# Modulation sums of a two-layer decoder trunk: four placed at the norms, a section's products moved into the mixer of layer 0

## The reference, cut to what matters

```python
c_act = jax.nn.silu(c)
for l in range(DEPTH):                       # DEPTH = 2
    mod = (c_act @ ada_w[l] + ada_b[l])[:, None, :]
    sh1, sc1, g1, sh2, sc2, g2 = jnp.split(mod, 6, axis=-1)
    h = rmsnorm(x, norm_mix_w[l]) * (1.0 + sc1) + sh1
    x = x + g1 * hybrid_mixer(h, ...)        # w_in, three branches with sigmoid gates, merged @ w_o
    h = rmsnorm(x, norm_ffn_w[l]) * (1.0 + sc2) + sh2
    ffn = swiglu(h, ...) if l % 2 == 0 else moe_swiglu(h, ...)   # top 2 of 8 experts
    x = x + g2 * ffn
return rmsnorm(x, final_norm_w)
```

## Time and profile before

| | |
|---|---|
| median of 3 runs | 1588.82 us (1588.61 to 1588.83) |
| the profiled execution | 1589.61 us, span 1586.9 us |
| busy: PE, PEld, DVE, ACT, POOL | 96%, 83%, 82%, 60%, 2% of the span |
| mean granted TensorE clock | 0.978 of full speed |
| DMA | 469.00 MB, mean 296 GB/s |
| stages by PE's matmuls | mixer 0 to 308 us, dense FFN to 520, mixer 1 to 789, experts to the end |

### The profile page before, as it was taken

One profiled execution on the slowest core, in us unless ns is written; L12 is line 12 of the kernel. 1 busy time (PEld: TensorE's weight loads), 2 busy tenths in 40 slices (PEclk: granted clock), 3 DMA queues, 4 the chain that ended last, 5 costly groups with the idle time before them and its releaser, 6 DMA issues.

```text
span 1586.9 us, 26455 instructions
## 1 busy us (share of the span) xinstructions
PE 1528.8 (96%) x9638; PEld 1322.0 (83%) x9638; DVE 1294.7 (82%) x1508; ACT 957.9 (60%) x1104; POOL 39.5 (2%) x46
## 2 busy tenths in 40 slices
PE   6899999899999899999889999999999999999997
PEld 5898999899999898999877777777777777777775
DVE  7776878767764878868669989899899998989897
ACT  3434544444433533544368777787878777787784
POOL 0000000000000000000002000000000000000200
PEclk7899999999999999999979999999999999999999
DMA  9943878468976543789549999999999999999993
GB/s 348 295 143 107 264 254 287 152 194 293 305 300 196 167 144 128 259 287 375 194 124 385 395 388 396 383 377 370 382 364 388 372 379 381 363 386 368 392 391 147
DMA packets 260624, 469.00 MB, mean 296 GB/s; under 512 B 15732, under 2 KB 129580, under 8 KB 260548
## 3 DMA queue, kind: packets, MB, share of 16 engines
q1 hardware_dynamic: 257024, 456.75, 81.3%
q0 software_dynamic: 3248, 11.11, 1.9%
q10 hardware_dynamic: 276, 0.09, 0.0%
HBM read 453.90 MB, written 14.00 MB: 295 GB/s over the span
## 4 chain that ended last, share of the span: by engine, by line
PE 75%; DVE 4%; issue 1%; ACT 0%; DVEq 0%
PE psU L621 52%; PE psA L621 22%; PE psA L1033 1%; DVE split L1332 1%; DVE merged L1441 0%; PE psU L971 0%; PE psU L993 0%; DVE rstd L1437 0%; DVE split L1813 0%; DVE adacc L1404 0%; DVE sc L1567 0%; DVE work L1635 0%; DVE work L2017 0%; DVE work L1551 0%; DVE work L1544 0%
## 5 line engine op out<-in xcount | busy, mean ns | idle before, releaser
L1116 ACT ACTIVATE split<-raw 128x1024 fp32r<-128x1024 f32 x754 | 787.5, 1059 | 364.8 <-PE psU L621 180.3
L1813 DVE TENSOR_TENSOR split<-raw,split 128x1024 fp32r<-128x1024 f32 x528 | 615.2, 1219 | 22.7 <-ACT split L1116 20.7
L621 PE MATMUL psU<-hS,split 128*128 128x256 f32 x3936 | 490.2, 287 | 18.1 <-DVE hS L1518 14.7
L621 PEld LDWEIGHTS psU<-hS,split 128*128 128x128 f32 x3936 | 483.5, 195 | 20.9 <-issue 16.8
L621 PE MATMUL psU<-split,xE 128*104 128x512 f32 (+1 forms) x2304 | 498.1, 376 | 2.3 <-DVE xE L1940 2.3
L621 PEld LDWEIGHTS psU<-split,xE 128*104 128x104 f32 x2304 | 366.9, 168 | 120.2 <-issue 2.4
L1332 DVE TENSOR_TENSOR split<-raw,split 128x1024 fp32r<-128x1024 f32 x226 | 268.8, 1218 | 67.3 <-ACT split L1116 66.9
L621 PE MATMUL psA<-split,hidE 128*104 128x512 f32 x1056 | 249.2, 395 | 0.0
L621 PEld LDWEIGHTS psA<-split,hidE 128*104 128x104 f32 x1056 | 175.4, 168 | 63.9
L1404 DVE SCALAR_TENSOR_TENSOR adacc<-raw,cact,adacc 128x1024 f32<-128x1024 f32 x70 | 89.7, 1281 | 4.1
L621 PE MATMUL psU<-yS,split 128*128 128x256 f32 x576 | 70.1, 283 | 0.0
(11 more groups left out here) (241 smaller groups left out, 806.8 us busy)
## 6 DMA issues: line engine op xcount, KB each, us to landing
raw<-in_moe_w_dram SPq DMA_DIRECT2D x528, 512.0 KB, 7.0
raw<-in_w_in_dram SPq DMA_DIRECT2D x120, 512.0 KB, 5.9
raw<-in_ada_w_dram SPq DMA_DIRECT2D x96, 512.0 KB, 7.1
raw<-in_ffn_w_dram SPq DMA_DIRECT2D x66, 512.0 KB, 6.4
raw<-in_w_o_dram SPq DMA_DIRECT2D x16, 512.0 KB, 9.1
token_rows<-sc SPq DMA_DIRECT2D x10, 512.0 KB, 9.5
raw<-in_w_br_a_dram SPq DMA_DIRECT2D x8, 512.0 KB, 8.7
raw<-in_w_br_c_dram SPq DMA_DIRECT2D x8, 512.0 KB, 9.2
```

The costliest lines, as they stand in the source:

```text
L621: return pe.matmul(o, a, b, start=start, stop=stop, skip_group_check=True)
L1116: return act.activation(o, i, ACT.Copy)
L1813: TTN(split[:, slot, 1, :], raw[:, (RAW0 + n) % RAW, :], split[:, slot, 0, :].bitcast(F32), ALU.subtract).then_inc(s_lo, 1)
```

## The change

It moves products and sums of the modulation; the values computed stay the same, and so does the number of pieces, products and sums.

- Pieces and products: the eight pieces of section 3 now stand between the pieces of branch a's gates in layer 0, those of 4 beside branch c, those of 5 beside branch b, instead of 3 beside c and 4 beside b. Section 5 has its own accumulator (`ada1`, a part of `work`), so its products wait for no sum. The FFN keeps sections 6 and 7, two products for each of eight pairs.
- Sums in layer 0: that of 2 stands behind the first gate unit of branch a, that of 3 behind `ya`; none is left behind `yc` or ahead of `w_o`. That of 4 stands between `stat_sum` and `stat_pair` at the second norm, that of 5 right behind `stat_pair`.
- In layer 1 the sum of section 10 stands between `stat_sum` and `stat_pair` too. That of 11 stands behind the statistics of layer 1's first norm instead of behind tile 17 of the FFN's second half. The `modulate` steps follow their sums.
- In layer 0 DVE no longer makes the low parts of all of branch a's gates ahead of `branch_low`: they stand between the products of section 3, as in the other branches.

```diff
-FFN_ADA = [5, 6, 7]
+STALL_ADA = 5
+FFN_ADA = [6, 7]
...
-FFN_TAKE = [3, 3, 2] * 3 + [0, 0]
+FFN_TAKE = [2] * 8 + [0, 0, 0]
...
-            ada = section() if b != BRANCHES[0] else []
+            ada = section() if l == 0 or b != BRANCHES[0] else []
...
                     for gg in range(2):
-                        for _ in project(lambda j: (l, "gate" + b, 2 * gg + j)):
-                            pass
+                        for j in project(lambda j: (l, "gate" + b, 2 * gg + j)):
+                            if (l, n, gg, j) == (0, 0, 0, 0):
+                                ada_sum(2)
...
-                    if n < 2:
+                    if l and n < 2:
                         ada_sum(6 * l + 2 + n)
+                    elif n == 0:
+                        ada_sum(3)
...
-                ada_sum(6 * l + 4)
+                scale, _ = open_event(("ada", 6 * l + 4))
                 stat, _ = open_event((l, "norm2"))
...
                 stat_sum(stat, l)
+                ada_sum(6 * l + 4, scale)
                 stat_pair(stat, 2 * l + 2, 3)
+                if l == 0:
+                    ada_sum(STALL_ADA)
...
                     down(f, w, range(KD)).then_inc(s_used, 1)
-                    if f == MOD_AT - 1:
-                        ada_sum(DOWN_ADA[0])
...
                 for jj in range(2, 4):
                     stat_pair(stat, 3, jj)
+                ada_sum(DOWN_ADA[0])
...
                 if second:
                     low_parts(SIGNAL[l, "wo", 3][2] + AHEAD)
+                    modulate(6 * l + 4)
...
                     gates = SIGNAL[(l, "gate" + BRANCHES[n], 0)][2] - 2
                     for k in ks:
-                        if n:
-                            low_parts(gates + k + 1)
-                        product(6 * l + 2 + n, k)
-                ada_part(0, range(4, KD))
+                        low_parts(gates + k + 1)
+                        product((3 if l == 0 else 6 * l + 2) + n, k)
+                for k in range(4, KD):
+                    product(6 * l + 2, k)
...
-                low_parts(SIGNAL[l, "gatea", 3][2])
+                if l:
+                    low_parts(SIGNAL[l, "gatea", 3][2])
...
-                branch_low(0)
-
                 for n, b in enumerate(BRANCHES):
-                    if n:
+                    if n or l == 0:
                         ada_part(n, range(4))
-                        branch_low(n)
+                    branch_low(n)
+                    if n or l == 0:
                         ada_part(n, range(4, KD))
```

More of the change, by code:

```diff
@@ L78 @@
 BANKWISE = NF - LAST_ROWS
-MOD_AT = 18
 DOWN_TAKE = [int(f % 2 == 0 and f < 2 * KD) for f in range(NF)]
 assert sum(DOWN_TAKE) == KD * len(DOWN_ADA)
-FFN_TAKE = [3, 3, 2] * 3 + [0, 0]
+FFN_TAKE = [2] * 8 + [0, 0, 0]
 assert sum(FFN_TAKE) == KD * len(FFN_ADA)
@@ L128, in event_plan @@
         if l == 0:
-            plan += [(("ada", s), "D") for s in FFN_ADA]
+            plan += [(("ada", s), "D") for s in [STALL_ADA] + FFN_ADA]
             plan += [("down0", "D"), ("down1", "D")]
@@ L160, in unit_signals @@
             direct += 1
-            used += MOD_AT if kind == "mod" else 0
+            used += NF if kind == "mod" else 0
             signal[key] = ("direct", direct, used)
-            used += NF - MOD_AT if kind == "mod" else 0
     return signal, used
@@ L682, in stat_sum, with ada_sum @@
                 mm(bank[:, 0:T], ones[:, :], sig[:, 0, 0:T], True, False)
-            def ada_sum(s):
+            def ada_sum(s, bank=None):
                 pe.wait_ge(s_afree, ADA_DONE[s])
-                bank = open_unit(("mod", s)) if s in DOWN_ADA else open_event(("ada", s))[0]
+                if bank is None:
+                    bank = open_unit(("mod", s)) if s in DOWN_ADA else open_event(("ada", s))[0]
+                acc = ada1 if s == STALL_ADA else adacc
                 for k in range(KD):
-                    last = mm(bank[:, k:k + 1], adacc[:, k * P:(k + 1) * P], ones[:, 0:1], True, True)
+                    last = mm(bank[:, k:k + 1], acc[:, k * P:(k + 1) * P], ones[:, 0:1], True, True)
                 last.then_inc(s_unit if s in DOWN_ADA else s_ev, 1)
@@ L1394, in product @@
                 dve.wait_ge(s_raw[pos % RAW], 16 * (pos // RAW + 1))
+                acc = ada1 if s == STALL_ADA else adacc[:, :]
                 if k == 0:
-                    if s > 1:
-                        last = [t for t in ADA_ORDER if t != 1]
+                    if s not in (0, STALL_ADA):
+                        last = [t for t in ADA_ORDER if t not in (1, STALL_ADA)]
                         last = last[last.index(s) - 1]
@@ L1588, in mixer @@
                     norm(l, 0)
+                    modulate(DOWN_ADA[0])
                     for k in range(4):
@@ L1735, in mixer @@
                         modulate(6 * l + 2 + n)
-                modulate(6 * l + 4)
                 dve.wait_ge(s_eD, emptied(EVENTS, EVENT_AT[("ada", 6 * l + 2)], "D"))
@@ L1760, in ffn_low @@
                 TTN(hid_lo[f], sig[:, f % 4, T:2 * T], hid_hi[:, f, :].bitcast(F32), ALU.subtract).then_inc(s_flo, 1)
+            modulate(STALL_ADA)
             done = 0
@@ L1783, in _ @@
                     done += 1
-            modulate(DOWN_ADA[0])
             dve.wait_ge(s_eD, emptied(EVENTS, EVENT_AT[("ada", 5)], "D"))
```

4 lines of the change are left out of this document (2 added, 2 removed).

## The result

| | before | after |
|---|---|---|
| median of 6 runs | 1588.82 us (1588.23 to 1590.01) | 1595.53 us (1594.48 to 1597.40) |
| profiled execution, its span | 1589.61, 1586.9 us | 1595.61, 1593.9 us |
| mean granted clock | 0.978 | 0.973 |

The ratio is 1.0043, with a 95% interval of 1.0031 to 1.0054. The changed kernel is slower by 6.7 us. In the two profiled executions the span is longer by 7.0 us and the device time by only 6.0: 1.7 us lie outside the span here and 2.7 did before. It is 1.71 to 1.81 us in every timed execution of the changed kernel and of the experiments, and 2.15 to 2.80 us in the executions of the kernel before that were timed beside the experiments. Which edit makes it shorter is open.

A forecast was written before the change was run, and what follows sets the result against it. PE, busy for 96% of the span, was taken as the bound. Terms: -8.5 for sums off its path, +1.0 at norms, +15.3 in branch a, +2.2 for the clock: +10.0 us, median 1598.8 us, range 1592.5 to 1602.5.

The forecast's parts named there:

- Step 1: Branch a, layer 0: ACT copies gate piece 2 only at 170.10, after its DMA; sigmoid and roots follow, ending at 175.65.
- Step 2: Branch a: DVE's reciprocal starts at 175.7, all behind it 4.9 us late; the second read of `o` ends at 186.25.
- Step 3: Branch a: PE waits 8.9 us for the bank of `o`; the sum of section 2 then takes 3.4 us at 1.2 GHz.
- Step 4: Branch a: gate piece 4's low part is ready 9.9 us after the sum of section 2 ends, at 199.65.
- Step 5: Branch a: `gatea` 1 ends at 196.1, PE waits 3.6 us, and `gatea` 2 starts at 199.7: 15.3 us lost.
- The second clock loss: Branch a: after PE's wait ahead of `gatea` 2 the clock is low again: 2.2 us lost.
- Sums off the path: From `gatea` 2 on, five sums instead of ten on PE's path, 1.70 us each: 8.5 us gained.
- The norms: Sums 4 and 10 between `stat_sum` and `stat_pair` make the last statistics 0.5 us late at each of two norms: 1.0 us lost.
- Rival 1: Branch a: ACT isn't held by gate piece 2's DMA; total +5.0, 1593.8 us; chance 0.08.
- Rival 3: At two norms: sums in the waits keep the clock up, 4.8 us back; total +5.2, 1594.0 us; chance 0.14.
- Rival 2: At `gatea` 2: gate piece 4's low part is there when PE arrives; -5.8 us, 1583.0 us; chance 0.07.
- Rival 4: Norm chain late by a whole sum at each place, ACT's wait in branch a 0.8 longer; +13.2, 1602.0 us; chance 0.09.

The follow-up runs named there:

- experiment 9: The changed kernel with 34 extra matmuls of 128 columns in branch a's wait ahead of the sum of section 2: 1595.62 us, ratio to before 1.0036.
- experiment 4: The changed kernel with the sum of section 2 as a unit in `psU`, not in the bank of `o`: 1595.48 us, ratio to before 1.0037.
- Experiment 3: The changed kernel with branch a's first four gate pieces together and section 3's pieces in twos behind the last four: 1587.10 us.
- experiment 7: The kernel before with only sums 4, 10, 11 moved to the norms, plus 14 and 10 extra matmuls in two norm waits: 1581.68 us.
- experiment 6: The kernel before with sums 4, 10, 11 at the norms, 4 and 10 in a second accumulator, sums 3 and 9 behind the last statistics: 1582.40 us.
- experiment 8: The kernel before with sums 4, 10, 11 at norms, layer 0's sum 3 behind the last statistics, 10 and 10 extra matmuls in norm waits: 1577.60 us.
- experiment 5: The changed kernel with branch a's first four gate pieces ahead of section 3's and the sum of section 2 in `psU`: 1586.13 us.
- experiment 1: The kernel before with only the sums of sections 4, 10 and 11 moved to the norms: 1583.63 us, ratio to before 0.9965.

## Why the prediction came out, point by point

The forecast was +10.0 us, 1598.8 us; measured are +6.7, 1595.53 us: inside the range, slower as forecast, and 3.3 us too high. In the traces the whole changed program is 0.9 us ahead of the old one when branch a begins (DVE multiplies `UB` at 158.26 instead of 159.17), which no part of the change explains. It belongs to that execution: experiment 9, the same program up to there, has 159.43, and experiment 4 has 157.83. The times of the changed kernel's trace below allow for it.

- **Step 1 of branch a, ACT: right.** It waited 10.12 us for the DMA of gate piece 2 and copied at 169.22; with the 0.9 that is the 170.10 of the forecast. Experiment 3 takes this away, and ACT's long wait for a DMA ahead of the input of branch a with it, by the order of DMAs, and 7.2 us of the 15.4 go.
- **Step 2, DVE: right.** The reciprocal began at 174.81 (175.7 in the old frame, as forecast) and the second read of `o` ended at 185.36 (forecast 186.25, or 185.35 here).
- **Step 3, PE: right.** The wait ahead of the sum was 9.00 us (forecast 8.9), the sum took 3.4 (forecast 3.4). PE stood still although the low part of gate piece 2 was ready: DVE made it and its neighbour from 181.28 to 183.57, and PE began only at 185.51. The bank of `gatea` 1 was free too, since experiment 9 writes into it from 177.52 on. So matmuls did not pass the waiting sum here. That agrees with the rule of the Trainium skill that I had weighed ("PSUM — Partial Sum Buffer", section Engine vs sequencer instructions).
- **Step 4, DVE again: right.** From the sum's end to the low part of gate piece 4 it was 9.9 us: 188.91 to 198.80 (197.58 + 1.22).
- **Step 5, PE again: the sum of the two right, its parts not.** `gatea` 2 began at 198.94, 15.4 us late; forecast was 15.3. But `gatea` 1 took 8.33 us (10.03 from its start to the next minus the wait of 1.70) instead of 6.3, since the clock stayed at 1.2 GHz for 8.7 us, and not 5, after PE resumed. So the wait ahead of `gatea` 2 was 1.7 us and not 3.6.
- **The second clock loss: the failed step.** The term "2.2 us lost" was 0: after 1.7 us of waiting the clock was still 1.00 (197 to 199), and `gatea` 2 and 3 took their full-speed 11.74. I had taken the size of a loss from one row and the wait from another part of my own sum, and the first clock loss, by stretching `gatea` 1, shortened the wait on which I had hung the second. The size was too large as well: at the wait of 2.70 us in the kernel before, the clock is low from 451 to about 454.4 (0.89 from 454 to 456), which is 1.7 us and not 2.2, and experiment 9 has 1.5 behind 2.73 us. That the clock held because the wait was shorter is argued from these three waits and not shown: in experiment 7 it fell although the last waits were only 1.90 and 0.55 us.
- **Sums off the path: right.** From `gatea` 2 to w_o it is 94.1 us (198.94 to 293.07) where it was 97.5 (184.4 to 281.87): two sums of 1.7. From the FFN to the router three sums go, less the 0.5 of a norm: the lag of PE falls from 11.7 us (324.65 against 312.93) to 8.6 at the first norm of layer 1 (533.24 against 524.63) and 7.7 at the router (800.42 against 792.71), 4.0 in all; forecast 4.6. The 0.6 that is missing is about what the clock takes: behind the second norm of layer 0 it was back 6.1 us after 324.65 and not 5.0 (0.56 from 329 to 331), and behind the first norm of layer 1 5.7 us after 533.24 and not 4.9. The last 0.7, to the span's 7.0, lies behind the router, where nothing changed.
- **The norms: 0.33 us instead of 0.5** at the second norm of layer 0. The term "1.0 us lost" for two norms was a little too large.
- **Cover of the sum ahead of w_o: nearly nothing, as said.** w_o takes 23.31 us (293.07 to 316.38) instead of 23.12. The sum behind `yc`: no wait in branch b of layer 0, as said; experiment 6 shows that the same sum in layer 1, which the change leaves alone, does cover 1.4 us.
- **Rivals.** 1 and 3 fall: ACT was held, and the clock was 0.50 at the second norm from 322 to 329. Rival 3's idea is right with more work in the wait (experiments 7 and 8); a sum alone was too little. Rival 2, that the cover holds in branch a, falls even with the DMAs in the better order and the bank free (experiments 3 and 5): what is left is DVE's load. Rival 4 falls at the norms (0.33 and not 1.7 each); there was no longer wait of ACT.

Put together, for the two traces: 10.0 as forecast, less 2.2 for the clock loss that was not there, less the 0.9 by which that execution was ahead, gives 6.9 beside 7.0 in the spans. The 0.9 can't explain the medians. There the second term is the time outside the span: the forecast added the longer span to the time whole, but this time fell from about 2.4 us (the median of the kernel before beside the experiments) to 1.76. An estimate from these is 10.0 - 2.2 - 0.7 = 7.1 beside 6.7. That the remaining small misses (0.33 for 0.5 at a norm, w_o, the clock behind the norms) nearly cancel is luck.

## What to carry to other kernels

Before work goes into a wait of the busiest engine, look at which engine that wait is for: at the norms PE waited for DVE and could take the sums for 0.33 us; in branch a DVE had no room, and the eight products moved there cost 15.4 us as built and 6.5 at best (experiment 5, the sum of section 2 in both). The norms' part alone comes out lower: 1583.6 us against 1586.1. Moving a piece in a list that several engines read in order moves it for all of them: the place of gate piece 2 among the DMAs cost 7.2 us by way of ACT and DVE, and the wait was seen at a bank that had little to do with it. Where two clock losses may follow each other, work them out in sequence: the first stretches the work ahead of the second wait and so shortens that wait.

## What the runs showed of the hardware

- How long the clock stays low after PE resumes varies widely in these traces. With projections first it was back 3.4 us after 311.84 (experiment 1), 4.0 us after 182.25 (experiment 4: 0.50 until 186, 0.93 from 186 to 188), 5.0 us after 312.93 and 6.1 us after 324.65 (changed kernel). With the one-column matmuls of a sum first it took 8.7 us after 185.51 in the changed kernel and 6.3 us after 181.61 in experiment 3 (0.78 from 187 to 189). The 8.7 us are the longest here, but their wait of 9.0 us is the longest too, and no run separates the two.
- The clock can fall while PE's records show it busy without a gap: in experiment 8 at 308.7, after sum, statistics, sum and the first of the extra matmuls. "TensorE: Matmul & The Clock Gate" in the Trainium skill, Part 1, What's actually happening, ties the clock to how busy PE has been recently. The long waits of this kernel agree with that; this stretch, recorded as busy at 1.00 from 306 to 309, does not, if busy is what the records count.
- Single executions of these kernels lie up to 6 us apart (experiment 5: 1584.59 to 1590.77 in 11 runs). Where the scatter arises was not followed up; the changed kernel's trace has 0.9 us ahead of branch a and 0.7 behind the router that no edit explains. So a profiled execution can lie 2 to 3 us off its kernel's median, as in experiments 3 (1589.35 against 1587.10) and 8 (1580.44 against 1577.60).
